# A ring of 12 step-function tiles, and the latent softmax's keys for two heads in one tile

## The reference

```python
def hybrid_layer(x, ...):                      # l = 0, 1
    proj = rms_norm(x, norm_g) @ w_in          # 1024 -> D_IN, split in 16 parts
    y_a = stick_breaking_attention(sa_q, sa_k, sa_v)           # 8 heads of 64
    q_b = (rms_norm(c_q, q_norm_g) @ w_uq)     # 8 heads x (64 + 32)
    kv_b = (rms_norm(c_kv, kv_norm_g) @ w_ukv) # 8 heads x (64 key + 64 value)
    k_b = concat([k_nope, broadcast(k_pe)])    # one 32-wide k_pe for all heads
    q_b, k_b = rms_norm(q_b, mla_q_g), rms_norm(k_b, mla_k_g)  # over 96
    # rope on the last 32 of each, then a causal softmax
    y_b = causal_softmax_attention(q_b, k_b, v_b, 96 ** -0.5)
    y_c = dsa_attention(...)   # top-128 keys by an index score; logits + bias
    # bias = rel_bias[t5_bucket(pq - pk)], 32 buckets, the same in both layers
    up = einsum(stack([y_a*silu(z_a), y_b*silu(z_b), y_c*silu(z_c)]), w_branch)
    return x + sum(sigmoid(g + gate_b) * up) @ w_out
```

## Time and profile before

| What | us |
|---|---|
| Median of 3 runs | 1355.99 (1354.79 to 1357.29) |
| Profiled execution: whole time | 1359.52 |
| Profiled execution: span | 1357.8 |
| TensorE busy | 1288.7 (95%) |
| VectorE busy | 771.8 (57%) |
| ScalarE busy | 609.0 (45%) |
| GpSimd busy | 192.1 (14%) |
| Step matmuls L787 before which TensorE idles for VectorE's tiles | 6.9 |
| TensorE idle before L978, for the squares | 8.7 |

### The profile page before, as it was taken

How to read it: one execution, slowest core, us unless ns; L and a number is a source line. 1 busy time by engine, 2 the same in 40 slices (tenths; PEclk the granted TensorE clock), 3 DMA queues, 4 the chain that set the end, 5 groups by cost and what they waited for, 6 DMA issues and landing times.

```text
span 1357.8 us, 17878 instructions
## 1 busy us (share of the span) xinstructions
PE 1288.7 (95%) x6538; PEld 966.7 (71%) x6538; DVE 771.8 (57%) x1572; ACT 609.0 (45%) x1131; POOL 192.1 (14%) x316
## 2 busy tenths in 40 slices
PE   6899899999889999999999999999988999999998
PEld 5546666655558888888888776665655888888887
DVE  5675777778663234354446667787865423434442
ACT  4234656666573223233334455666667322223330
POOL 1234211123440000000000021112344000000000
PEclk9899899999999999999999999999999999999999
DMA  7244111100241222223332311110024122332321
GB/s 215 78 117 87 63 63 32 47 32 1 82 137 57 99 93 93 94 93 108 109 70 86 93 63 63 32 47 32 1 88 132 63 96 91 102 112 83 107 94 62
DMA packets 118568, 109.15 MB, mean 80 GB/s; under 512 B 34512, under 2 KB 101200, under 8 KB 118480
## 3 DMA queue, kind: packets, MB, share of 16 engines
q1 hardware_dynamic: 118480, 107.99, 26.1%
HBM read 100.64 MB, written 7.34 MB: 80 GB/s over the span
## 4 chain that ended last, share of the span: by engine, by line
PE 75%; DVE 9%; ACT 8%; issue 5%; POOL 1%; SPq 1%; DMA 1%; ACTq 0%; DVEq 0%
PE bank L832 20%; PE bank L833 19%; PE bank L834 19%; PE bank L978 3%; PE bank L1146 2%; PE bank L787 2%; DVE w_lo L724 2%; PE bank L1189 2%; PE bank L1173 2%; ACT w_hi L718 1%; PE bank L1002 1%; ACT soft L1477 1%; DVE probs L2039 1%; ACT soft L1479 1%; PE bank L1019 1%
## 5 line engine op out<-in xcount | busy, mean ns | idle before, releaser
L832 PE MATMUL bank<-h_hi,w_hi 128*128 128x512 f32 (+1 forms) x928 | 362.7, 391 | 3.9 <-DVE w_lo L724 2.1
L834 PE MATMUL bank<-h_hi,w_lo 128*128 128x512 f32 (+1 forms) x928 | 353.9, 381 | 0.0
L833 PE MATMUL bank<-h_lo,w_hi 128*128 128x512 f32 (+1 forms) x928 | 353.9, 381 | 0.0
L724 DVE TENSOR_TENSOR w_lo<-raw,w_hi 128x2048 fp32r<-128x2048 f32 (+2 forms) x98 | 187.8, 1918 | 120.2 <-ACT w_hi L718 120.2
L832 PEld LDWEIGHTS bank<-h_hi,w_hi 128*128 128x128 f32 x928 | 177.0, 191 | 50.9 <-issue 12.6
L718 ACT CAST w_hi<-raw 128x2048 fp32r<-128x2048 f32 (+2 forms) x100 | 159.1, 1593 | 112.2 <-PE bank L834 110.1
L834 PEld LDWEIGHTS bank<-h_hi,w_lo 128*128 128x128 f32 x928 | 176.8, 191 | 33.5
L833 PEld LDWEIGHTS bank<-h_lo,w_hi 128*128 128x128 f32 x928 | 177.1, 191 | 33.0 <-issue 2.2
L1661 ACT ACTIVATE gate<-bank,gains 128x512 f32<-128x512 f32 x48 | 33.0, 688 | 166.1 <-PE bank L834 166.1
L2224 POOL TENSOR_SCALAR probs<-probs,stat 128x128 f32<-128x128 f32 (+3 forms) x128 | 75.5, 591 | 151.0 <-DVE stat L1994 144.9
L832 PE MATMUL bank<-br_hi,w_hi 128*128 128x512 f32 x192 | 74.7, 389 | 0.0
(11 more groups left out here) (231 smaller groups left out, 2160.4 us busy)
## 6 DMA issues: line engine op xcount, KB each, us to landing
raw<-in_w_in SPq DMA_DIRECT2D x56, 1024.0 KB, 5.0
raw<-in_w_branch SPq DMA_DIRECT2D x12, 1024.0 KB, 5.1
raw<-in_w_out SPq DMA_DIRECT2D x8, 1024.0 KB, 5.0
bias<-bias_dram SPq DMA_DIRECT2D x16, 256.0 KB, 3.0
bias<-bias_dram SPq DMA_DIRECT2D x16, 192.0 KB, 2.5
x_sb<-in_x SPq DMA_DIRECT2D x4, 512.0 KB, 4.5
bias_dram<-bias_out SPq DMA_DIRECT2D x8, 256.0 KB, 2.9
raw<-in_w_in SPq DMA_DIRECT2D x4, 512.0 KB, 4.6
```

Of the source, the lines that this page charges most:

```text
L724: e.tensor_tensor(w_lo[:, s % RING, a:b], raw[:, s % RAW, a:b], w_hi[:, s % RING, a:b].bitcast(F32), ALU.subtract).then_inc(*lo_signal(nam ...
L832: pe.matmul(out_ap, lh, rh, start=start and i == 0, stop=False)
L833: pe.matmul(out_ap, lh, rl, start=False, stop=False)
L834: mm = pe.matmul(out_ap, ll, rh, start=False, stop=stop and i == n - 1)
```

## The change

It has four parts.

1. **Ring of 12.** Four more tiles (reach_q, reach_k) in the space of sa_q and sa_k; tile g waits for tile g - 12. take_f moves to another place, and so VectorE copies big_eye and causal out of it before the first tiles. VectorE's `reaches` are written one group further ahead from the third group on, and the last ones stand ahead of the w_lo of slab 4.
2. **Slab 5** is rounded by ScalarE after the first group of relus instead of the third, and its w_lo stands ahead of score unit 4 instead of 12.
3. **Sine and first rope**: the sine with its table loads stands ahead of the copies of sa_v, and `first_rope` ahead of step 0 instead of in step 1. It and its counterpart in layer 1 also copy the rope part of k to rows 0 to 63.
4. **Keys for two heads**: tile kp{p} has the keys of heads 2p (rows 0 to 63) and 2p + 1 (rows 64 to 127), w_ukv being loaded with all keys first and then all values. One square, one norm with `per_head` (which sums over each half of the rows), one log and exp serve both. The squares of k_pe stand in a tile of their own (k_pe_sq, in both halves), which GpSimd adds to the squares. k_head becomes a ring of 4. The two logits banks change places.

The diff, cut:

```diff
-            if g >= 8:
-                e.wait_ge(*bias_mm.of(0, g - 8))
+            if g >= REACH_RING:
+                e.wait_ge(*bias_mm.of(0, g - REACH_RING))
...
@@ loads
-                    return [(slot[:, 0:HEADS * P], w_ukv[l])]
+                    src = w_ukv[l].rearrange("p (h n) -> p h n", h=HEADS)
+                    v = slot[:, 0:HEADS * P].rearrange("p (c h n) -> p c h n", c=2, h=HEADS)
+                    return [(v[:, c, :, :], src[:, :, c * HD:c * HD + HD]) for c in range(2)]
...
@@ TensorE
+                def prep_k(p):
+                    if p == 0:
+                        use("ukv")
+                    b = tile_bank(f"kp{p}")
+                    two = slice(2 * p * NOPE, (2 * p + 2) * NOPE)
+                    three(b[:, :], [(ukv[0][:, two], ukv[1][:, two], ckv_hi[:, :], ckv_lo[:, :])]
+                          ).then_inc(*dense.tick(f"kp{p}"))
...
+                def norm_k(p):
+                    pe.wait_ge(*pool_work.at(f"kp{p}sq"))
+                    pe.wait_ge(*act_evac.at(f"qh{2 * p - 1 if p else 0}ln"))
+                    norm(f"kp{p}", per_head, kp_sq)
...
+                    if i >= 2:
+                        pv_of(i - 2)
                     if i == STEPS + 1:
                         norm_k(0)
-                    if i >= 2:
-                        pv_of(i - 2)
...
-                    if h + 1 < HEADS:
-                        if t == 0:
-                            prep_k(h + 1)
-                        if t == 2 and h + 2 < HEADS:
-                            prep_q(h + 2)
+                    if h % 2 == 0 and t == 0 and h + 2 < HEADS:
+                        prep_k(h // 2 + 1)
+                    if t == 2 and h + 2 < HEADS:
+                        prep_q(h + 2)
                     if i >= T_LAG:
                         t_of(i - T_LAG)
...
-                        if t == 1:
-                            norm_k(h + 1)
-                        if t == 3 and h + 2 < HEADS:
-                            norm_q(h + 2)
+                    if h % 2 == 0 and t == 2 and h + 2 < HEADS:
+                        norm_k(h // 2 + 1)
+                    if t == 3 and h + 2 < HEADS:
+                        norm_q(h + 2)
...
@@ ScalarE
-                e.activation(k_sq[64:96, :], dbank("k_pe")[64:96, :], ACT.Square).then_inc(*act_evac.tick("k_pe"))
+                e.activation(k_pe_sq[0:32, :], dbank("k_pe")[64:96, :], ACT.Square).then_inc(*act_evac.tick("k_pe low"))
+                e.activation(k_pe_sq[64:96, :], dbank("k_pe")[64:96, :], ACT.Square).then_inc(*act_evac.tick("k_pe"))
...
                     index_relus(0)
+                    hi(5)
                     index_relus(1)
                     index_relus(2)
-                    hi(5)
...
+                def sq_k(p):
+                    e.wait_ge(*dense.at(f"kp{p}"))
+                    if p:
+                        e.wait_ge(*norm_sum.at(f"kp{p - 1}"))
+                    e.activation(kp_sq[:, :], dbank(f"kp{p}")[:, :], ACT.Square).then_inc(*act_evac.tick(f"kp{p}sq"))
...
+                    if h + 2 < HEADS:
+                        if h % 2 == 0 and t == 0:
+                            sq_k(h // 2 + 1)
+                        if t == 2:
                             sq_q(h + 2)
+                        if h % 2 == 0 and t == 2:
+                            rs_k(h // 2 + 1)
+                        if t == 3:
                             rs_q(h + 2)
...
@@ VectorE
-                    reaches(e, 3, 6)
+                    reaches(e, 3, 7)
                     ix_q_parts(0)
                     split_lo(e, SLABS[2])
-                    reaches(e, 6, 10)
+                    reaches(e, 7, 11)
                     ix_q_parts(1)
-                    reaches(e, 10, G_AT["ix_q1"][1])
...
-                    reaches(e, *G_AT["sa_k0a"])
+                    reaches(e, G_AT["sa_k0a"][0] + 1, G_AT["sa_k0a"][1] + 1)
+                    copy_parts(e, 7)
+                    reaches(e, G_AT["sa_k0b"][0] + 1, GROUPS)
                     split_lo(e, SLABS[4])
-                    copy_parts(e, 7)
-                    reaches(e, G_AT["sa_k0b"][0], GROUPS)
...
-                    if layer.l == 0 and u == 12:
+                    if layer.l == 0 and u == 4:
                         split_lo(e, SLABS[5])
...
-                        if t == 2:
-                            head_k(h + 1)
+                    if h % 2 and h + 1 < HEADS and t < 2:
+                        head_k(h + 1 + t)
...
@@ GpSimd
+                def squares_k(p):
+                    e.wait_ge(*act_evac.at(f"kp{p}sq"))
+                    e.tensor_tensor(kp_sq[:, :], kp_sq[:, :], k_pe_sq[:, :], ALU.add).then_inc(*pool_work.tick(f"kp{p}sq"))
+                    e.wait_ge(*pool_work.at(f"kp{p}sq"))
...
+                        if br == "mla" and h + 2 < HEADS and h % 2 == 0 and t == 1:
                             e.wait_ge(*probs_normed.at(i - 1))
+                            squares_k(h // 2 + 1)
+                        if br == "mla" and h + 1 < HEADS and h % 2 and t < 2:
+                            e.wait_ge(*probs_normed.at(i - 1))
+                            rope_k(h + 1 + t)
```

147 lines of the change are left out of this document (72 added, 75 removed).

## The result

| | before | changed |
|---|---|---|
| median of 12 runs each | 1354.88 us (1353.41 to 1357.29) | 1359.61 us (1354.74 to 1361.96) |
| ratio of the two, 95% interval | | 1.003 (1.0019 to 1.0042) |
| profiled execution: whole time, span | 1359.52, 1357.8 us | 1354.74, 1352.8 us |
| mean granted clock, profiled execution | 0.991 | 0.992 |

The change makes the kernel 0.3% slower; the forecast was 1326 us. The difference is small, but its interval lies above 1. The profiled execution of the changed kernel is its fastest run: the other eleven took 1356.9 to 1362.0 us with a mean granted clock of 0.984 to 0.988. Its trace shows where the time went, but about 5 us of a usual run's loss are not in it. The profiled execution of the kernel before lies 4.6 us above the median of its runs, so the two traces taken alone would say that the change gains 5 us.

What follows compares the result with a forecast made beforehand. TensorE, busy 95%, was the bound, losing time in four places. Terms 13 + 3.3 + 4 + 10 = 30.3 us took 1359.52 to 1329.2; with medians 3.5 lower, 1326 us, range 1319 to 1333 (8 in 10: 1316 to 1340).

Steps and rivals of the forecast that it cites:

- The four places: Where TensorE gives time away: bias table, sixth slab's load split, start of layer 0's stick-breaking, latent softmax of both layers.
- Part 1, 13 us: Bias table: the ring of 12 removes most waits for step tiles; 13 us won, bounds 5 and 19.
- Part 2, 3.3 us: Index scores: earlier rounding and w_lo of the sixth slab remove a wait and slow products; 3.3 us, bounds 0 and 4.6.
- Part 3, 4 us: Start of layer 0's stick-breaking: earlier sine and first rope win 4 us, bounds 0 and 8.1.
- Part 4, 10 us: Latent softmax: keys for two heads win 5 us a layer, 10 us for both; bounds -4 and 16.
- the unit-by-unit reckoning: Latent softmax, per layer: 0.35 us lost, 1.9 + 1.4 + 1.4 + 1.7 won, 6 us; taken as 5 with bubbles.
- the named signs of being wrong: In the changed profile: table stage over 68 us, softmax stages at 73 us, or clock below 1.00 in mid-softmax.
- The norm's wait for GpSimd: Latent softmax: GpSimd's sum done 1.2 us after TensorE reaches the norm, three times a layer.
- Rival (b): Latent softmax gives nothing, as the norm's wait for GpSimd eats the matmuls saved; 20 us won, 1336 us; chance 0.15.
- (d): Softmax: TensorE idles over 2 us at each pair's norm for GpSimd's sum, clock falls; +30 us, 1366 us; chance 0.03.
- that rule: Softmax: VectorE operations with two SBUF inputs lock GpSimd's shared port; sum of squares may wait, 4 us, 1330 us; left out.

Runs made afterwards that it cites:

- keys per head: Parts 1 to 3 of the change without part 4, keys made head by head as in the kernel before: 1337.56 us, ratio 0.9871.
- the early kernel: Changed kernel with both k_head products and both rope halves of a pair moved to the even head's last unit: 1336.24 us, ratio 0.9859.
- the last version: The early kernel with norms behind the v_b products and ScalarE's query square ahead of the third unit's exponential: 1331.24 us, ratio 0.9811.
- part 4 alone: Kernel before with only keys for two heads added; ring of 8, slab 5, sine and first rope as before: 1374.89 us, ratio 1.0147.

## Why the prediction was wrong

- **What bounds the kernel.** The four places were the right ones. All gains came from them.
- **Part 1, 13 us.** Right: 13.8 us alone. Step matmuls and their waits fell from 40.5 us to 27.2 (21.77 busy, 3.4 and 2.0 waited), where I had written 28. The slots came nearly as reckoned: the second still waits (3.42 us), and the sixth takes 3.16 us where the seventh, as wide, takes 2.07, so 1.1 us of its time is a wait drawn as busy, for which I had left 0.9. The others, apart from the first, have none. (The ten gains add up to 14.3, not 14.2.) The step matmuls' busy time in the stage, and the two waits that are left:

```profile
33.10:98.30 65.20, 21.77 (x256) 8.18 (x256) 0.95 0.40 114
```

```profile
36.15 0.94 PE L799 MATMUL bank<-reach_v,step_w 128*32 128x128 f32 x8 [2.02 <-DVE reach_v L513]
45.62 0.71 PE L799 MATMUL bank<-reach_u,step_w 128*32 128x128 f32 x8 [3.42 <-DVE reach_u L513]
```

- **Part 2, 3.3 us.** Too high: about 0, its lower bound ("the wait only moves to the scores"). The wait and its slow products behind the earlier trace rows did go, but a wait for ScalarE's relu (2.00 us at 107.76) stands in its place, with slow products behind it. The place was foreseen, VectorE's w_lo ahead of the fifth score, and priced at 2.3 us of VectorE and up to 0.8 of TensorE. It took 3.38 us beside GpSimd's angle product; the 1.1 us more and the 0.8 would make 1.9 of the 2.00.
- **Part 3, 4 us.** Right within its bounds, 2 to 3 us. The waits of 3.03 and 1.86 us of the earlier trace rows went, and a wait of 2.41 us for the copies of sa_v came, ahead of the stage's first matmul, where I had up to 2.3 us; the three make 2.5 us. The new waits of parts 2 and 3:

```profile
107.76 0.50 PE L909 MATMUL bank<-ix_k_parts,ix_q_parts 128*128 128x512 f32 x1 [2.00 <-ACT ix_relu L1391]
128.00 0.49 PE L1004 MATMUL bank<-sa_q,sa_k 64*128 64x128 f32 x4 [2.41 <-ACT sa_v L1446]
```

- **Part 4, 10 us.** This is the step that failed: it costs 20 us instead, and the place is the unit-by-unit reckoning, in which "each later pair wins 1.4 us". I counted every matmul, the chain of squares and VectorE's order, and wrote that the two k_head products now stand "one after the other at the start of the odd head", but did not ask what that read of the key tile holds back. It holds a bank, and the odd head's query product wants it. Two of the named signs of being wrong came with it: softmax stages over 73 us, and a clock below 1.00 inside them. The norm's wait for GpSimd, which I priced at 1.2 us three times a layer, is 0.71 us twice in each softmax and 0.87 once ahead of it.

  The bank is not all of it. With its wait gone, part 4 is worth 1.3 us (1336.2 against 1337.6, whose intervals overlap), not 10, and the kernel is still 10 us above the forecast. In the traces each softmax stage is 2.3 us shorter than with keys per head (68.3 against 70.6), and 0.7 to 0.8 us comes back in each stick-breaking stage, whose last norm waits 0.87 us for GpSimd's sum (0.46 for the squares with keys per head), and 0.9 us between the layers, of which 0.7 is a new wait for norm_out that I can't explain. TensorE has 4.9 us less to do in the stage than with keys per head (I had counted 6.2), but it waits longer: 6.9 us in all in layer 0 of the early kernel (the five rows under that run and two small ones), where keys per head have 3.9 for the squares and 0.3 for the values. The prediction had let the waits for squares shrink. With these shortened too (the last version), the stage is 66.0 us. The 68.3 us of the early kernel are the 68.5 that I had written, but by luck: I came from 73.6 us, a window 1.3 us too long with a stretch of lower clock in it (0.98 in the earlier trace rows), and keys per head at a clock of 1.00 take 70.6.
- **Rival (b), 1336 us.** This is where the kernel stands once the bank's wait is gone: parts 1 to 3 nearly whole, and new waits in place of the matmuls saved. Its waiter was the norm behind GpSimd's sum; in layer 0 that is 0.8 us, and ScalarE's squares and roots are 3.7.
- **The rival on the slower side, (d),** had the right kind of price (a wait of 2 to 3 us for each of six, and slow products behind) and the wrong waiter. Its 5 us each came as some 4, since not every wait takes the clock. I gave it 0.03 because I asked only whether the norm could wait that long.
- **GpSimd against VectorE.** The trace shows the conflict: 1.37 us for VectorE's product beside GpSimd's 1.28, 0.69 alone. By the Trainium skill ("SBUF — State Buffer", section "Who interferes with whom") the shared ports are an exclusive lock between these two engines. The trace agrees: the product always ends 0.55 us behind GpSimd's, about as if it had only begun then. The prediction had weighed that rule only for GpSimd as the one that waits. It left it out because GpSimd's key products "beside the same products" were never longer, and that was a misreading: in the kernel before, not one of them runs beside q_head's second product. The sum of squares did meet that product, twice a layer, but GpSimd was first and VectorE waited (1.64 us). GpSimd's rope halves beside the next three lengthened two of the fatal waits by 0.4 to 0.6 us, and GpSimd's angles lengthened w_lo by 1.1. What the sum and the angles cost in time there was not tested.

So 20.3 us forecast for parts 1 to 3 came as 17.3. On top of them part 4, forecast to win 10, costs 22 (1337.6 to 1359.9 us). The bank's wait with its clock is 23.7 of these 32, and the new waits in place of the saved work are most of the rest.

## What to carry to other kernels

When a tile is merged or its place in a ring changes, write the new order of tiles beside the ring's depth, and for every tile name the last reader of the one whose buffer it takes, and where that reader stands in its engine's queue; do it for the products that the change doesn't mention as well. A read that is put off costs nothing on its own engine and can cost 3 us on another, six times over. If such a wait turns up, move the read ahead, not the product back: here that turned +0.3% into -1.4% with no work removed. Where two engines' instructions newly stand side by side, look up each one's length beside the other in the trace before pricing it alone. And let each part be timed alone where a change has several: a gain of 17 us and a loss of 20 looked like no change.

## What the runs showed of the hardware

- Waits of TensorE can cost more than their length: by the medians 8.2 us less of them gave 15 us, and 19.3 us less gave 23.7, where two executions of equal clock differ by 18.3. In the changed kernel the mean granted clock went with the time from 0.992 (1354.3 us) to 0.982 (1362.8 us) in runs of one and the same program. In the traces of the changed kernel (two) and of part 4 alone, the clock fell at all six waits of 3.6 us and at one of the twelve of 3.0 to 3.1. It also fell behind shorter ones elsewhere, such as the 2.00 us at 107.76.
- The stretch of the bias table, the same instructions in all kernels with the ring of 12, took 62.2 us in the executions in which the clock stayed at 1.00 and 65.9 where it was 0.92; a difference of 3 us in one stage of single executions proves nothing there.
- A product of 64x512 on VectorE, both inputs in SBUF, takes 0.69 us alone. It takes 1.01 to 1.37 us beside a GpSimd product of the same shape and 1.63 to 1.65 beside one of 128x512, and ends 0.55 us behind it each time. A subtraction of 128x2048 on VectorE (w_lo) takes 2.29 us alone and 3.38 beside a GpSimd product that started 0.11 us ahead of it.
